# A second FFN input copy that carries the token roots, and right halves copied out of PSUM by ScalarE

## The reference

```
def rms_norm(x, g):
    y = x32 * lax.rsqrt(jnp.mean(x32 * x32, axis=-1, keepdims=True) + NORM_EPS)
    return y * g

def conv_gated_mlp(h, w_up, conv_w, w_down):       # h (256, 1024), w_up (1024, 5632)
    u = h @ w_up
    u = sum(pad(u)[t:t + S] * conv_w[t] for t in range(3))      # along the tokens
    gate, val = split(u)
    return (gelu(gate) * val) @ w_down                          # w_down (2816, 1024)

h = rms_norm(x, ffn_pre_norm[l])
x = x + rms_norm(conv_gated_mlp(h, w_up[l], ffn_conv[l], w_down[l]), ffn_post_norm[l])
```

## Time and profile before

| | |
|---|---|
| median of 3 runs | 1029.5 us (1029.44 to 1029.59) |
| span of the profiled execution | 1027.2 us, mean granted TensorE clock 0.999 |
| time of the profiled execution beside its span | not recorded apart; the runs' median is 2.3 us above the span |
| FFN of layer 0 | up0 starts at 328.07 us, the last down piece ends near 515.6 us |
| DMA | 170.78 MB, mean 166 GB/s |

### The profile page before, as it was taken

One profiled execution on the slowest core, in us unless ns is written; L12 is line 12 of the kernel. 1 busy time (PEld: TensorE's weight loads), 2 busy tenths in 40 slices (PEclk: granted clock), 3 DMA queues, 4 the chain that ended last, 5 costly groups with the idle time before them and its releaser, 6 DMA issues.

```text
span 1027.2 us, 15935 instructions
## 1 busy us (share of the span) xinstructions
PE 1013.0 (99%) x6244; PEld 908.5 (88%) x6244; DVE 680.7 (66%) x932; ACT 587.5 (57%) x859; POOL 130.7 (13%) x257
## 2 busy tenths in 40 slices
PE   8999999999999999999999999999999999999997
PEld 7889999888888999999888899998888889999996
DVE  5635566655596887878865355666555869787877
ACT  5657666565446654555575666565653457455553
POOL 3353124000002000000025221230000020000000
PEclk9999999999999999999999999999999999999999
DMA  8554345444444646555454534464344645545551
GB/s 259 178 177 155 122 141 168 161 165 164 144 150 157 203 169 203 170 200 172 168 190 159 174 124 128 150 205 164 124 144 164 204 145 166 203 169 201 174 195 41
DMA packets 109037, 170.78 MB, mean 166 GB/s; under 512 B 3377, under 2 KB 72804, under 8 KB 108964
## 3 DMA queue, kind: packets, MB, share of 16 engines
q1 hardware_dynamic: 107676, 166.88, 48.8%
q10 hardware_dynamic: 1208, 2.63, 0.7%
q0 software_dynamic: 80, 0.26, 0.1%
HBM read 168.72 MB, written 1.05 MB: 165 GB/s over the span
## 4 chain that ended last, share of the span: by engine, by line
PE 95%; DVE 1%; ACT 1%; DMA 1%; issue 1%; DVEq 0%; SPq 0%; POOL 0%; POOLq 0%
PE bank L1418 28%; PE bank L1420 28%; PE bank L1419 28%; PE bank L1783 2%; PE bank L1684 1%; PE bank L1705 1%; PE bank L1776 1%; PE bank L1693 1%; PE bank L1721 1%; PE bank L1728 1%; PE bank L1773 1%; DMA w_raw<-in_w_in_dram 1%; PE bank L1735 1%; PE bank L1741 1%; DVE x_rows L1233 0%
## 5 line engine op out<-in xcount | busy, mean ns | idle before, releaser
L1053 DVE TENSOR_TENSOR w_lo<-w_raw,w_hi 128x2048 fp32r<-128x2048 f32 (+3 forms) x174 | 364.3, 2094 | 160.6 <-ACT w_hi L700 160.5
L700 ACT ACTIVATE w_hi<-w_raw 128x2048 fp32r<-128x2048 f32 (+3 forms) x174 | 304.7, 1752 | 50.3 <-PE bank L1420 48.8
L1418 PE MATMUL bank<-w_hi,hT_lo 128*128 128x512 f32 (+2 forms) x700 | 258.4, 369 | 1.5 <-DVE hT_lo L1127 0.8
L1420 PE MATMUL bank<-w_hi,hT_hi 128*128 128x512 f32 (+2 forms) x700 | 252.9, 361 | 0.0
L1419 PE MATMUL bank<-w_lo,hT_hi 128*128 128x512 f32 (+2 forms) x700 | 252.5, 361 | 0.0
L1418 PE MATMUL bank<-hT_hi,w_lo 128*128 128x256 f32 x704 | 199.4, 283 | 0.7 <-DVE hT_lo L1080 0.7
L1420 PE MATMUL bank<-hT_hi,w_hi 128*128 128x256 f32 x704 | 199.2, 283 | 0.0
L1419 PE MATMUL bank<-hT_lo,w_hi 128*128 128x256 f32 x704 | 199.2, 283 | 0.0
L1418 PEld LDWEIGHTS bank<-w_hi,hT_lo 128*128 128x128 f32 x700 | 131.5, 188 | 17.8 <-issue 3.0
L1420 PEld LDWEIGHTS bank<-w_hi,hT_hi 128*128 128x128 f32 x700 | 131.4, 188 | 14.1
L1419 PEld LDWEIGHTS bank<-w_lo,hT_hi 128*128 128x128 f32 x700 | 131.6, 188 | 13.0
(11 more groups left out here) (215 smaller groups left out, 1250.1 us busy)
## 6 DMA issues: line engine op xcount, KB each, us to landing
w_raw<-in_w_up_dram SPq DMA_DIRECT2D x44, 1024.0 KB, 4.9
w_raw<-in_w_in_dram SPq DMA_DIRECT2D x36, 1024.0 KB, 4.9
w_raw<-in_w_in_dram SPq DMA_DIRECT2D x36, 768.0 KB, 4.2
w_raw<-in_w_down_dram SPq DMA_DIRECT2D x22, 1024.0 KB, 4.8
w_raw<-in_w_out_dram SPq DMA_DIRECT2D x8, 1024.0 KB, 4.9
w_raw<-in_w_in_dram SPq DMA_DIRECT2D x8, 672.0 KB, 4.0
w_raw<-in_w_branch_mla_dram SPq DMA_DIRECT2D x4, 1024.0 KB, 4.9
w_raw<-in_w_branch_diff_dram SPq DMA_DIRECT2D x4, 1024.0 KB, 4.8
```

The lines of the kernel that those rows point to most:

```text
L700: nc.scalar.activation(w_hi[:, n % RING, 0:nk * cols], raw[:, n % RING, 0:nk * cols], ACT.Copy).then_inc(hi_done, 1)
L1053: V.tensor_tensor(w_lo[:, n % RING, s], raw[:, n % RING, s], w_hi[:, n % RING, s].bitcast(F32), ALU.subtract).then_inc(lo_done, 1)
L1418: PE.matmul(dst, lhs[1], rhs_hi, start=start, stop=False)
L1420: return PE.matmul(dst, lhs[0], rhs_hi, start=False, stop=stop)
```

## The change

From the seventh up piece on (c >= 6, `SCALED`), TensorE streams another copy of the input, `scaled`, in which for each k the high and the low part of the scaled input stand side by side in 512 columns. The copy holds (hT_hi + hT_lo) x token_scale, split anew. It is made once a layer: GpSimd adds and multiplies 128 x 2048 in the buffer `merged` (free by then), ScalarE makes the high part at the step of up3, GpSimd subtracts for the low part. For each (j, k) there are two matmuls: the high weights against all 512 columns, and the low weights against the left 256. So each half j takes a bank of its own and a piece two banks; the four banks hold two pieces. The left half of a bank has low x high + high x high, the right half high x low. ScalarE copies the right halves (128 x 512) to `up_low`, and VectorE adds the left halves from PSUM; the roots are in already, so that add takes the place of the multiplication by `token_scale`.

```diff
--- before.py
+++ after.py
@@ -281,6 +281,9 @@
         out.append(c)
         rest -= c
     return out + [float(np.float32(rest))]
+
+
+SCALED = 6
 
 
 def lambda_init(layer):
@@ -368,11 +371,15 @@
             g_lo = sb("g_lo", [P, G_RING, 512], F32R, scope=four)
             square_ffn = sb("square_ffn", [P, D], scope=four)
             up_scaled = sb("up_scaled", [P, 2, 2, SEQ], scope=four)
+            scaled = sb("scaled_input", [P, KD, 2, SEQ], F32R, scope=four)
+            up_low = sb("up_low", [P, 2, SEQ], scope=four)
         with ExitStack() as six:
             sb("pad_six", [P, 5120], scope=six)
             par_rows = sb("par_rows", [44, 4 * DEPTH, P], scope=six)
 
-        bank = [ctx.enter_context(nc.psum_tensor(f"bank{i}", [P, 512], F32)) for i in range(8)]
+        bank = [ctx.enter_context(nc.psum_tensor(f"bank{i}", [P, 512], F32)) for i in range(4)]
+        high_banks = ctx.enter_context(nc.psum_tensor("high_banks", [P, 4, 512], F32))
+        bank += [high_banks[:, i, :] for i in range(4)]
         S_BANK, O_BANK = (bank[4], bank[5]), bank[7]
 
         def t_bank(n):
@@ -413,6 +420,8 @@
         squares, rstd_done = sem("squares"), sem("rstd_done")
         ffn_squares = sem("ffn_squares")
         root_rows_ready, scales_full, up_scaled_done = sem("root_rows_ready"), sem("scales_full"), sem("up_scaled_done")
+        scaled_whole, scaled_hi, scaled_lo = sem("scaled_whole"), sem("scaled_hi"), sem("scaled_lo")
+        up_low_copied = sem("up_low_copied")
         lat_squares, lat_normed = sem("lat_squares"), sem("lat_normed")
         attn_means, latent_means, latent_roots = sem("attn_means"), sem("latent_means"), sem("latent_roots")
         head_means, head_roots = sem("head_means"), sem("head_roots")
@@ -504,6 +513,11 @@
             return bank[4 + c % 4][:, j * SEQ:(j + 1) * SEQ]
 
         root_rows = xn[:, 0, 0:NT * P].rearrange("p (t q) -> p t q", t=NT)
+        def up_banks(c):
+
+            pair = (c + 1) % 2
+            return high_banks[:, 2 * pair:2 * pair + 2, :]
+
         token_scale = xn[:, 0, 512:512 + SEQ]
 
         def tile_tokens(cols, t):
@@ -665,6 +679,18 @@
                 for t in range(NT):
                     root(l, (0, t), post_squares, l * 8 + (t + 3), 4 + 2 * t)
                     root(l, ("pre", t), ffn_squares, l * 2 * NT + (2 * t + 2), 2 * t)
+
+                whole = merged[:].rearrange("p t (k q) -> p (t k) q", q=SEQ)
+                pool.wait_ge(turn_emptied, l * NTURN + (TURN_BEFORE["ffn"] + len(FFN_LO)))
+                nc.gpsimd.tensor_tensor(whole, hT_hi[:].bitcast(F32), hT_lo[:].bitcast(F32), ALU.add)
+                pool.wait_ge(up_scaled_done, l * 2 * NU + 1)
+                pool.drain()
+                nc.gpsimd.tensor_tensor(whole, whole, token_scale.rearrange("p (o q) -> p o q", o=1).broadcast_to([P, KD, SEQ]),
+                                        ALU.mult).then_inc(scaled_whole, 1)
+                pool.wait_ge(scaled_hi, l + 1)
+                pool.drain()
+                nc.gpsimd.tensor_tensor(scaled[:, :, 1, :], whole, scaled[:, :, 0, :].bitcast(F32), ALU.subtract).then_inc(scaled_lo, 1)
+
                 for t in range(NT):
                     root(l, (1, t), post_squares, l * 8 + (4 + 2 * t + 2), 4 + 2 * t)
 
@@ -941,6 +967,12 @@
                                 post_square(l, 0, t, 0)
                         if kind == "up":
                             u, b = c // 2, c % 2
+                            if c == 3:
+                                act.wait_ge(scaled_whole, l + 1)
+                                nc.scalar.activation(scaled[:, :, 0, :], merged[:].rearrange("p t (k q) -> p (t k) q", q=SEQ), ACT.Copy).then_inc(scaled_hi, 1)
+                            if c >= SCALED:
+                                act.wait_ge(piece_used, l * NPIECE + (RING + n + 1))
+                                nc.scalar.activation(up_low[:], up_banks(c)[:, :, SEQ:2 * SEQ], ACT.Copy).then_inc(up_low_copied, 1)
                             act.wait_ge(up_scaled_done, l * 2 * NU + (c + 1))
                             if b == 1 and u >= 2:
 
@@ -1102,9 +1134,12 @@
                     scale_rows(l)
                     for j in range(2):
                         last = V.tensor_tensor(up_scaled[:, c % 2, j, :], up_half(c, j), token_scale, ALU.mult)
-                else:
+                elif c < SCALED:
                     last = V.tensor_tensor(up_scaled[:, c % 2, :, :], bank[4 + c % 4][:].rearrange("p (j q) -> p j q", j=2),
                                            token_scale.rearrange("p (o q) -> p o q", o=1).broadcast_to([P, 2, SEQ]), ALU.mult)
+                else:
+                    dve.wait_ge(up_low_copied, l * (2 * NU - SCALED) + (c - SCALED + 1))
+                    last = V.tensor_tensor(up_scaled[:, c % 2, :, :], up_banks(c)[:, :, 0:SEQ], up_low[:], ALU.add)
                 last.then_inc(up_scaled_done, 1)
 
             def gated(l, u):
@@ -1419,6 +1454,15 @@
                 PE.matmul(dst, lhs[0], rhs_lo, start=False, stop=False)
                 return PE.matmul(dst, lhs[0], rhs_hi, start=False, stop=stop)
 
+            def passes_beside(dst, w_parts, k):
+
+                if k == 0:
+                    PE.matmul(dst, w_parts[0], scaled[:, k, :, :], start=True, stop=False)
+                last = PE.matmul(dst[:, 0:SEQ], w_parts[1], scaled[:, k, 0, :], start=False, stop=False)
+                if k:
+                    last = PE.matmul(dst, w_parts[0], scaled[:, k, :, :], start=False, stop=k == KD - 1)
+                return last
+
             def rows(hi, lo, k, t):
                 return hi[:, k, t * P:(t + 1) * P], lo[:, k, t * P:(t + 1) * P]
 
@@ -1493,9 +1537,14 @@
                 pe.wait_ge(lo_done, l * NPIECE + (n + 1 + RING))
                 if kind == "up":
                     u, b = c // 2, c % 2
-                    if c >= 4:
+                    if 4 <= c < SCALED:
 
                         pe.wait_ge(up_scaled_done, l * 2 * NU + (c - 3))
+                    if c == SCALED:
+                        pe.wait_ge(scaled_lo, l + 1)
+                        pe.wait_ge(up_scaled_done, l * 2 * NU + (c - 2))
+                    if c > SCALED:
+                        pe.wait_ge(up_scaled_done, l * 2 * NU + (c - 1))
                     order = [(k, j) for k in range(8) for j in range(2)] if c == 0 else [(k, j) for j in range(2) for k in range(8)]
                     for k, j in order:
                         if c == 0 and j == 0 and k % 2 == 0:
@@ -1503,8 +1552,11 @@
                             pe.wait_ge(turn_emptied, l * NTURN + (TURN_BEFORE["ffn"] + last_of + 1))
                         if c == 1 and (k, j) == (0, 1):
                             turn_roots(l)
-                        last = passes(up_half(c, j), (hi[:, k, j * P:(j + 1) * P], lo[:, k, j * P:(j + 1) * P]),
-                                      hT_hi[:, k, :], hT_lo[:, k, :], k == 0, k == 7)
+                        w_parts = (hi[:, k, j * P:(j + 1) * P], lo[:, k, j * P:(j + 1) * P])
+                        if c < SCALED:
+                            last = passes(up_half(c, j), w_parts, hT_hi[:, k, :], hT_lo[:, k, :], k == 0, k == 7)
+                        else:
+                            last = passes_beside(up_banks(c)[:, j, :], w_parts, k)
                     last.then_inc(piece_used, 1)
                     return
                 halves = 2 if cols == 1024 else 1
```

## The result

The changed kernel takes 1044.1 us (median of 4, 1043.7 to 1044.5) against 1029.5 us: ratio 1.0142, 95% interval 1.0128 to 1.0156, 14.6 us slower. 1043.2 was predicted. The profiled execution has a span of 1042.2 us, 15.0 more than before.

What follows compares the result with a forecast made beforehand. TensorE's stream was taken to bound the kernel: 1029.5 us, less 6.8 for matmuls, plus 1.7 at the layers' ends and 18.8 of stalls from GpSimd, gives 1043.2 us; range 1024 to 1051, the forecast mechanism's own 1038 to 1048.

Steps and rivals of the forecast that it cites:

- The three gaps: TensorE stalls before up2, up3 and up5 of each layer: 1.5, 4.8 and 3.0 us, VectorE being kept out by GpSimd.
- T: Time of one GpSimd instruction of 128x2048: 4.6 us, with ends of 2.3 and 7.4 us.
- The rival in which long instructions don't keep VectorE out: No split is late beside GpSimd's long instructions: 1024.4 us, or 1022.7 with cover at the layer's end; chance 0.24.
- step 1: GpSimd's add gets in ahead of VectorE's split of up2 and holds until 339.45: TensorE stalls 1.5 us.
- The multiply: GpSimd's second instruction, from 342.95 to 347.55, delays VectorE's taps and the split of up3: TensorE stalls 4.8 us.
- Step 3: GpSimd's subtract holds until 363.85, delaying VectorE's gating and the split of up5: TensorE stalls 3.0 us.
- the clock falls in the stalls: Rival: TensorE drops to 1.2 GHz after its stall, up to 5.8 us a layer, 1046 to 1055 us; chance 0.12.
- The matmuls: In 16 up pieces per layer, three 256-column matmuls become two, saving 13.3 ns each of 512 times: 6.8 us.
- The end of the layer: VectorE, 0.9 us later, makes the last g_lo late for the last down piece: about 0.85 us, twice, +1.7 us.
- The copy in mid-stage: ScalarE's 128x512 copy out of PSUM, 689 ns ahead of VectorE's add; g_lo keeps 0.7 us of cover, so free.

Runs made afterwards that it cites:

- x1: The kernel before plus only GpSimd's three instructions and ScalarE's copy of the high part, which no matmul uses: 1048.9 us, ratio 1.0186.
- x2: The changed kernel without GpSimd's three instructions; ScalarE copies hT_hi and hT_lo instead, so the roots are left out: 1025.87 us against 1029.66, ratio 0.9962.
- x5: The changed kernel with each GpSimd instruction cut in eight of 128x256: 1033.2 us, ratio 1.0042.
- x7: The changed kernel with add, multiply and subtract on VectorE in the first three down steps, new way only for c = 12 to 19: 1026.71 us, ratio 0.9972.
- x4: The changed kernel with 22 transposes of the identity before the wait for up3's weights, to keep TensorE's clock up: 1046.7 us.
- x3: The changed kernel with the last two up pieces of a layer (c = 20, 21) done as in the kernel before: 1043.65 us.
- x6: x2 with the eight 512-column matmuls of each half ahead of the eight 256-column ones: 1025.06 us against 1025.87.

## Why the prediction was right

- *The three gaps* were predicted at 9.4 us a layer (0.1 of it at down0) and are 9.1, and 0.1 from up5 to down0. The cause is shown by x1 and x2, and x5 and x7 agree. T = 4.6 us, worked out along 16 and 128 elements, is 4.55, 4.64 and 4.62. The rule of the Trainium skill ("SBUF — State Buffer", two separate sides), an exclusive lock held for the whole instruction, so far shown for 0.3 us, holds for an instruction fifteen times as long. The rival in which long instructions don't keep VectorE out is refuted.
- *Their places* were off. At step 1 the prediction let VectorE's small root instruction pass and stopped the split; its rule spoke only of instructions with two SBUF inputs, and this one has one. GpSimd came 0.07 us ahead of it and kept it out, so TensorE waited in the middle of up1 (2.5 us) rather than before up2 (1.5). (The split's end in that step was also added 0.09 us short: 339.45 + 2.29 is 341.74, not 341.65; 341.80 was measured.) The multiply began at 343.20, 0.25 us after its time, and the split of up3 ended at 352.3 (352.2 said). But TensorE had begun up2 1.4 us later than said (343.07 for 341.65), so it waited 3.5 us instead of 4.8. The two waits together, 6.0 us, were 6.3 in the prediction: when up3 can start is set by VectorE's schedule, wherever TensorE waits before it.
- *Step 3*: 1.5 us instead of 3.0. The clock had fallen and up3 took 1.6 us longer; that time was the missing part of the wait. The rival "the clock falls in the stalls" was right as to the event (chance given 0.12) and wrong as to its price: it adds nothing while VectorE is the one being waited for. It was sized as an addition to the gaps; in x4, x1 and x3 only a fall at up5's start or behind it adds, 1.4 to 1.5 us. That neither fall of the profiled execution came there was luck: the prediction's sum had the clock kept.
- *The matmuls*: sized 6.8 us, measured 32 x 0.165 = 5.3 in the up pieces and 0.03 us in each of the seven down pieces between them, so 5.6 in all. A pair takes some 350 instead of 346.7 ns, which goes with the changes of width (x6). One instruction saved is thus worth some 11 ns, not 13.3. The prediction held against this the N/2.4 + 2.5 ns of the Trainium skill ("TensorE: Matmul & The Clock Gate", Back-to-back issue gap) as the figure for a stream. That section calls it the gap of an isolated matmul and gives 131 ns at 512 columns for a stream of weight loads and matmuls; neither 2.5 ns nor 131 fits this kernel, with 11 and 227.
- *The end of the layer*: 1.7 us said, 1.6 measured (0.8 a layer), most of it before down10 and 0.2 before down9. x3 shows that the last two pieces make it.
- *The copy in mid-stage*: free, as said; down1 to down7 take 5.44 us. It takes 0.60 us, not 0.69. The trace of before had this price: it has copies of 128x512 out of PSUM without a second operand (L774, 596 ns), and the prediction took a row with one.

So part of the closeness is luck. The gain was 1.2 us too large and the gaps 0.4 us too large, which partly cancel, and 0.4 us ahead of the first FFN was not forecast. In the profiled executions the difference is 15.0 us where 13.7 was said; in the medians it is 14.6, and 0.9 remain.

## What to carry to other kernels

Before moving work to an idle GpSimd, look at what VectorE has queued at that moment: in this kernel a GpSimd instruction on SBUF kept VectorE's next SBUF instruction out for its whole length, so its price was its duration less the slack of the tightest thing behind VectorE, once per instruction. An engine that is 13% busy was no free resource here; an idle stretch of VectorE was, at half the duration. If it has to be GpSimd, cut the instruction into short ones (x5: 1033.2 for 1044.1 us).

When TensorE and VectorE wait for each other in turn, as here, add up the schedule of the one that is late; gaps and slow stretches of the other ahead of the meeting point are the same time, and not to be summed.

## What the runs showed of the hardware

- A VectorE instruction with one SBUF input and an SBUF output (128x128, tensor_scalar) was kept out too: 4.56 for 0.28 us. One with a PSUM and an SBUF input was not: 0.69 us inside GpSimd's subtract.
- The clock fell after TensorE had stood idle for 3.3 us in the changed kernel, and in x1, x3 and x4 after 1.9, 2.3, 2.5 and 2.8 us; after 2.3 us in up1 of the changed kernel it did not fall. Each time it stayed at the 1.2 GHz level for 3.4 us, nearly all of it with TensorE busy, and a piece in it took 1.5 to 1.6 us longer.
- In the fp32r stream a 256-column matmul costs 120 ns and a 512-column one 227. Mixed, a pair costs some 350: behind a change from 256 to 512 columns the distances are longer, in the kernel before too (233, 236, 228, 233 and 231 ns at the head of a down piece).
